# Expert retrieval of a diffusion block: 32 tokens times four expert ranks in a slot, and the V sum through 128x32 factors

## The reference, cut to what matters

```python
scores = jnp.einsum("blhtd,htkd->blhtk", q, sub_keys)
sv, si = lax.top_k(scores, PEER_TOPK)
cand_s = (sv[..., 0, :, None] + sv[..., 1, None, :]).reshape(b, L, PEER_HEADS, n_cand)
cand_i = (si[..., 0, :, None] * N_KEYS + si[..., 1, None, :]).reshape(b, L, PEER_HEADS, n_cand)
top_s, pos = lax.top_k(cand_s, PEER_TOPK)
idx = jnp.take_along_axis(cand_i, pos, axis=-1)
gate = jax.nn.softmax(top_s, axis=-1)
...
act = jax.nn.gelu(jnp.einsum("tkd,td->tk", u_tab[it], xt))
return jnp.einsum("tk,tkd->td", gt * act, v_tab[it])
```

## Time and profile before

| | |
|---|---|
| times of three runs | 5720.74, 5721.03, 5723.74 us, median 5721.03 |
| the profiled execution | 5723.5 us of span, and nothing of its time is listed outside it |
| PE busy | 4492.1 us, 78% |
| DVE busy | 3507.4 us, 61% |
| POOL busy | 2171.7 us, 38% |
| ACT busy | 1461.2 us, 26% |
| gathers (queue 0) | 1342.26 MB of 1549.20 MB moved |
| PE products of line 1510 | 5120 passes, 2619.8 us |

### The profile page before, as it was taken

How to read it: one execution, slowest core, us unless ns; L and a number is a source line. 1 busy time by engine, 2 the same in 40 slices (tenths; PEclk the granted TensorE clock), 3 DMA queues, 4 the chain that set the end, 5 groups by cost and what they waited for, 6 DMA issues and landing times. The chain is left out here.

```text
span 5723.5 us, 53344 instructions
## 1 busy us (share of the span) xinstructions
PE 4492.1 (78%) x15560; PEld 2613.2 (46%) x15560; DVE 3507.4 (61%) x7342; ACT 1461.2 (26%) x3249; POOL 2171.7 (38%) x1631
## 2 busy tenths in 40 slices
PE   9778979867777877777777777978986777777776
PEld 3677867743333533333333235777862333333332
DVE  1555565456666456666766667747336666666766
ACT  0244343222211312221222223334221222222222
POOL 0345323344444334444444443333323444444443
PEclk9888989888888888888888887898988888888888
DMA  8423202289999379999999992101219999999998
GB/s 310 150 82 116 74 1 96 89 312 386 371 385 378 151 309 383 378 384 382 377 386 380 384 384 102 61 30 67 81 63 382 383 378 382 382 387 383 385 384 330
DMA packets 232302, 1549.20 MB, mean 271 GB/s; under 512 B 39877, under 2 KB 41157, under 8 KB 45893
## 3 DMA queue, kind: packets, MB, share of 16 engines
q0 software_dynamic: 184320, 1342.26, 59.5%
q1 hardware_dynamic: 47818, 204.82, 10.3%
HBM read 1544.79 MB, written 2.20 MB: 270 GB/s over the span
## 5 line engine op out<-in xcount | busy, mean ns | idle before, releaser
L1510 PE MATMUL banks<-arena 128*128 128x512 f32 x5120 | 2619.8, 672 | 913.6 <-ACT arena L1486 913.1
L1419 POOL DMA_INDIRECT arena<-in_experts,arena x1280 | 1455.6, 1137 | 2114.5 <-PE banks L1510 1855.0
L1510 PEld LDWEIGHTS banks<-arena 128*128 128x128 f32 x5120 | 1077.7, 216 | 2457.0 <-issue 1288.4
L1450 DVE CUSTOM_DVE_ANT_0 arena<-arena 128x1024 f32<-128x1024 f32 x1280 | 1538.8, 1224 | 954.5 <-DMA arena<-in_experts,arena 925.5
L265 POOL TENSOR_TENSOR wide_low<-wide_blocks,wide_high 128x1024 fp32r<-128x1024 f32 x244 | 612.7, 2533 | 1182.3 <-ACT wide_high L255 1182.3
L1478 ACT ACTIVATE arena<-arena 128x4 f32<-128x4 f32 x320 | 66.1, 207 | 2659.4 <-DVE arena L1450 2659.4
L303 PE MATMUL banks<-activation_a,wide_high 128*128 128x512 f32 (+1 forms) x1568 | 582.9, 372 | 12.2 <-ACT arena L327 4.2
L305 PE MATMUL banks<-activation_a,wide_low 128*128 128x512 f32 (+1 forms) x1568 | 563.3, 359 | 0.0
L1486 ACT ACTIVATE arena<-identity,arena 128x128 f32<-128x128 f32 x1280 | 408.8, 390 | 100.2 <-DVE arena L1456 96.1
L304 PE MATMUL banks<-activation_b,wide_high 128*128 128x512 f32 (+1 forms) x1056 | 385.4, 365 | 0.0
L303 PEld LDWEIGHTS banks<-activation_a,wide_high 128*128 128x128 f32 x1568 | 308.7, 197 | 61.1 <-ACT arena L327 5.4
(11 more groups left out here) (176 smaller groups left out, 4576.6 us busy)
## 6 DMA issues: line engine op xcount, KB each, us to landing
wide_blocks<-in_wide SPq DMA_DIRECT2D x170, 1024.0 KB, 4.8
arena<-in_experts,arena POOLq DMA_INDIRECT x1280, 9.2
arena<-mod_rows SPq DMA_DIRECT2D x9, 512.0 KB, 5.4
residual<-in_tokens SPq DMA_DIRECT2D x6, 512.0 KB, 7.3
arena<-in_keys SPq DMA_DIRECT2D x3, 1024.0 KB, 7.2
arena<-in_icnt_grid SPq DMA_DIRECT2D x2, 1024.0 KB, 5.8
out_x<-residual SPq DMA_DIRECT2D x4, 512.0 KB
arena<-in_pool_w SPq DMA_DIRECT2D x3, 512.0 KB, 3.3
```

Of the source, the lines that this page charges most:

```text
L1419: pool.indirect_dma_start(out=v.ring[:, j % RING], out_offset=None, in_=io["experts"], in_offset=bass.IndirectOffsetOnAxis(ap=idx[:, par * ...
L1450: last = nc.vector.tensor_tensor_reduce(out=u_row, in0=u_row, in1=v.h2[:, t], scale=1.0, scalar=0.0, op0=ALU.mult, op1=ALU.add, accum_out= ...
L1510: mm = nc.tensor.matmul(k.ps[:, a + half], v.diag[:, j % 8], v.ring[:, j % RING, D + half * BANK:D + (half + 1) * BANK], start=False, stop ...
```

## The change

A slot no longer holds one rank of 128 tokens. It holds 32 tokens times four ranks: partition 32q + i of slot j in a group is token 32j + i with rank 4s + q, where s is the group. Group and unit counts stay: 16 gathers of 1 MB in a unit.

- **Token copies.** The dot product now needs the tokens of a slot repeated four times. PE makes these copies by products with slices of the identity (four 128x32 products of 512 columns for each of 8 half copies), ACT copies them from PSUM (`copies`), once for each tile: the first at the start of a stage, the next ones after the last group of a tile.
- **V sum.** The factor of a slot is 128x32: `masks` (a fold of the identity times the gates, made by POOL once for a unit) scaled by the Gelu on ACT. Slot j of a group writes PSUM partitions 32j to 32j + 31. For each half the four slots follow each other. One increment after the eight products frees all four slots. The zeroing and closing products (lines 1504 and 1515) go.
- **DVE** no longer multiplies gates and Gelu, and no longer waits for ACT after each group. The multiplication with the key numbers (line 1254) moves to POOL (`match`), after its fourth gather; `masks` stands after its eighth.
- **Numbers and gates in the new layout.** `spread` on PE brings them to the slot layout: 16 products 128x32 with 8 columns. It stands after the products of group 0 of each unit. Then `take_rows` on DVE writes the row indices of the next unit, right after the fourth dot product of group 0, and `take_gates` on ACT copies the gates.
- **Distance.** Choosing runs two units ahead instead of one: best keys after the sixth dot product, best pairs after the tenth, weights after the thirteenth. `stage_queries` chooses units 0 and 1.
- The loops are written out. The three rows loaded by SP have a place of their own in the arena. One more constant (`fold`) is loaded at the start.

```diff
-    ring, h2, scores, dg, small = carve(k, RING * 2 * D, 4 * D, 4 * 2048 + 256, 8 * P, 2000)
+    ring, h2, scores, lhs, small, rows = carve(k, RING * 2 * D, 4 * D, 4 * 2048, 8 * QUAD, 2080, 3 * D)
     v.ring = ring.rearrange("p (s c) -> p s c", s=RING)
     v.raw_ring = ring
     v.h2 = h2.rearrange("p (t c) -> p t c", t=4)
-    v.scores, v.g2, v.lng, v.lnb = scores, k.rows[:, 0], k.rows[:, 1], k.rows[:, 2]
-    v.diag = dg.rearrange("p (s c) -> p s c", s=8)
+    v.rows = rows.rearrange("p (n c) -> p n c", n=3)
+    v.scores, v.g2, v.lng, v.lnb = scores, v.rows[:, 0], v.rows[:, 1], v.rows[:, 2]
+    v.lhs = lhs.rearrange("p (q j c) -> p q j c", q=2, j=NJ)
...
+    def softmax(act, u):
+
+        act.wait_ge(k.top_ready.sem, b0["top_ready"] + u + 1)
+        nc.scalar.activation(raw, tv, ACT.Exp, bias=nmax, accum_out=esum).then_inc(k.soft_done.sem, 1)
+
+    def weigh(dve, u):
+
+        dve.wait_ge(k.soft_done.sem, b0["soft_done"] + u + 1)
         nc.vector.reciprocal(einv, esum)
         dve.drain()
-        g = gate[:, par * 16:par * 16 + 16]
-        nc.vector.tensor_scalar(g, g, einv, None, ALU.mult)
-
-    def softmax(act, par, unit):
-        act.wait_ge(k.top_ready.sem, unit + 1)
-        nc.scalar.activation(gate[:, par * 16:par * 16 + 16], tv, ACT.Exp, bias=nmax,
-                             accum_out=esum).then_inc(k.soft_done.sem, 1)
+        nc.vector.tensor_scalar(sel[:, u % 2, 1], raw, einv, None, ALU.mult)
+
+    def match(pool, u):
+
+        pool.wait_ge(k.picked.sem, b0["picked"] + u + 1)
+        nc.gpsimd.tensor_tensor(hot, hot, sif[:, u % 2].unsqueeze(1).to_broadcast(wide_shape), ALU.mult) \
+            .then_inc(k.matched.sem, 1)
+
+    def number(dve, u):
+
+        dve.wait_ge(k.matched.sem, b0["matched"] + u + 1)
+        nc.vector.tensor_reduce(sel[:, u % 2, 0], hot.rearrange("p s z b -> p s (z b)"), AX_X, ALU.add) \
+            .then_inc(k.chosen.sem, 1)
+
+    def spread(pe, u):
+
+        pe.wait_ge(k.chosen.sem, b0["chosen"] + u + 1)
+        if u >= 1:
+            pe.wait_ge(k.gate_copied.sem, b0["gate_copied"] + u)
+        for j in range(NJ):
+            for q in range(NJ):
+                last = nc.tensor.matmul(k.ps[q * QUAD:(q + 1) * QUAD, 7, j * 8:j * 8 + 8],
+                                        k.ident[:, j * QUAD:(j + 1) * QUAD], sel[:, u % 2, :, q * 4:q * 4 + 4],
+                                        start=True, stop=True)
+        last.then_inc(k.spread.sem, 1)
+
+    view = k.ps[:, 7, 0:NJ * 8].rearrange("p (j z s) -> p z s j", j=NJ, z=2)
+
+    def take_rows(dve, u):
+
+        dve.wait_ge(k.spread.sem, b0["spread"] + u + 1)
+        nc.vector.tensor_scalar(idx[:, u % 4], view[:, 0], float(layer * N_EXPERTS), None, ALU.add) \
+            .then_inc(k.idx_ready.sem, 1)
+
+    def take_gates(act, u):
+
+        act.wait_ge(k.idx_ready.sem, b0["idx_ready"] + u + 1)
+        if u >= 2:
+            act.wait_ge(k.masks_ready.sem, b0["masks_ready"] + u - 1)
+        nc.scalar.copy(gate[:, u % 2], view[:, 1]).then_inc(k.gate_copied.sem, 1)
+
+    def masks_of(pool, u):
+
+        pool.wait_ge(k.gate_copied.sem, b0["gate_copied"] + u + 1)
+        if u >= 1:
+            pool.wait_ge(k.lhs_ready.sem, b0["lhs_ready"] + 4 * u)
+        shape = [P, TOPK, QUAD]
+        nc.gpsimd.tensor_tensor(masks, k.fold[:].unsqueeze(1).to_broadcast(shape),
+                                bc(gate[:, u % 2].rearrange("p s j -> p (s j)"), shape), ALU.mult) \
+            .then_inc(k.masks_ready.sem, 1)
...
@@ stage_retrieve
+            for u in range(UNITS):
+                pool.wait_ge(k.idx_ready.sem, b0["idx_ready"] + u + 1)
+                for n in range(TOPK):
+                    g = u * TOPK + n
+                    if g >= RING:
+                        pool.wait_ge(k.slot_free.sem, b0["slot_free"] + (g - RING) // NJ + 1)
+                    pool.indirect_dma_start(
+                        out=v.ring[:, g % RING], out_offset=None, in_=io["experts"],
+                        in_offset=bass.IndirectOffsetOnAxis(ap=c.idx[:, u % 4, n // NJ, n % NJ:n % NJ + 1], axis=0),
+                    ).then_inc(k.landed[g % RING].sem, 16)
+                    if n == 3 and u >= 1 and u + 1 < UNITS:
+                        c.match(pool, u + 1)
+                    if n == RING - 1 and u >= 1:
+                        c.masks(pool, u)
...
-                            dve.wait_ge(k.gelus.sem, i * 8 + (q0 + t * 32 + par * 4 + q + 1))
-                            nc.vector.tensor_tensor(wgt[:, j - 3:j + 1], gel[:, j - 3:j + 1],
-                                                    gate[:, par * 16 + j - 3:par * 16 + j + 1], ALU.mult) \
-                                .then_inc(k.weights.sem, 1)
...
+            for u in range(UNITS):
+                t = u // PEER_HEADS
+                ahead = u + 2 < UNITS
+                for n in range(TOPK):
+                    g = u * TOPK + n
+                    if u % PEER_HEADS == 0 and n < NJ:
+                        dve.wait_ge(k.copy_ready.sem, k.copy_ready.at(t * 2 * NJ + 2 * n + 2))
+                    dve.wait_ge(k.landed[g % RING].sem, r0 + 16 * (g // RING + 1))
+                    if g >= 32 and n % NJ == 0:
+                        dve.wait_ge(k.lhs_ready.sem, b0["lhs_ready"] + (g - 32) // NJ + 1)
+                    u_row = v.ring[:, g % RING, 0:D]
+                    last = nc.vector.tensor_tensor_reduce(
+                        out=u_row, in0=u_row, in1=k.copies[:, n % NJ], scale=1.0, scalar=0.0,
+                        op0=ALU.mult, op1=ALU.add, accum_out=c.act_in[:, g % 32:g % 32 + 1])
+                    if n % NJ == NJ - 1:
+                        last.then_inc(k.dots.sem, 1)
+                    if n == 1 and u >= 1 and u + 1 < UNITS:
+                        c.number(dve, u + 1)
+                    if n == 3 and u >= 1 and u + 1 < UNITS:
+                        c.take_rows(dve, u + 1)
+                    if n == 5 and ahead:
+                        c.best_keys(dve, u + 2)
+                    if n == 9 and ahead:
+                        c.best_pairs(dve, u + 2)
+                    if n == 12 and ahead:
+                        c.weigh(dve, u + 2)
...
-                                nc.scalar.activation(v.diag[:, j % 8], k.ident[:], ACT.Copy,
-                                                     scale=wgt[:, j:j + 1]).then_inc(k.diags.sem, 1)
...
+            def copies(t):
+
+                for j in range(NJ):
+                    for half in range(2):
+                        n = (t * NJ + j) * 2 + half
+                        act.wait_ge(k.copy_proj.sem, k.copy_proj.at(n + 1))
+                        if t >= 1:
+                            act.wait_ge(k.dots.sem, b0["dots"] + t * PEER_HEADS * 4)
+                        nc.scalar.copy(k.copies[:, j, half * BANK:(half + 1) * BANK], k.ps[:, 4 + n % 2]) \
+                            .then_inc(k.copy_ready.sem, 1)
+
+            copies(0)
+            for u in range(UNITS):
+                t = u // PEER_HEADS
+                for q in range(4):
+                    g = u * 4 + q
+                    act.wait_ge(k.dots.sem, b0["dots"] + g + 1)
+                    a = (g % 8) * NJ
+                    nc.scalar.activation(c.gel[:, a:a + NJ], c.act_in[:, a:a + NJ], ACT.Gelu_apprx_tanh)
+                    if q == 0:
+                        act.wait_ge(k.masks_ready.sem, b0["masks_ready"] + u + 1)
+                    if g >= 2:
+                        act.wait_ge(k.slot_free.sem, b0["slot_free"] + g - 1)
+                    act.drain()
+                    for j in range(NJ):
+                        last = nc.scalar.activation(v.lhs[:, g % 2, j], c.masked[:, q * NJ + j], ACT.Copy,
+                                                    scale=c.gel[:, a + j:a + j + 1])
+                    last.then_inc(k.lhs_ready.sem, 1)
+                    if q == 0 and u >= 1 and u + 1 < UNITS:
+                        c.take_gates(act, u + 1)
+                    if q == 2 and u + 2 < UNITS:
+                        c.softmax(act, u + 2)
+                if u % PEER_HEADS == PEER_HEADS - 1 and t + 1 < NT:
+                    copies(t + 1)
...
-                        for half in range(2):
-                            mm = nc.tensor.matmul(k.ps[:, a + half], v.diag[:, j % 8],
-                                                  v.ring[:, j % RING, D + half * BANK:D + (half + 1) * BANK],
-                                                  start=False, stop=False, skip_group_check=True)
-                        mm.then_inc(k.slot_free.sem, 1)
...
+            def copies(t):
+
+                for j in range(NJ):
+                    for half in range(2):
+                        n = (t * NJ + j) * 2 + half
+                        if n >= 2:
+                            pe.wait_ge(k.copy_ready.sem, k.copy_ready.at(n - 1))
+                        for q in range(NJ):
+                            last = nc.tensor.matmul(k.ps[q * QUAD:(q + 1) * QUAD, 4 + n % 2],
```

(41 more changed lines are left out.)

222 lines of the change are left out of this document (89 added, 133 removed).

## The result

The changed kernel takes 5951.85 us (median of 4 runs, 5944.67 to 5952.71), the one before 5720.89; the ratio is **1.0405**, 95% interval 1.039 to 1.0419.

What follows compares the result with a forecast made beforehand. The prediction took a slot's way from row landed to slot free as the bound, not PE's work. A unit of 54.2 us against 43.9 gave 5723.5 + 762 + 24 + 90 + 15, about 6620 us; range 6000 to 7300.

Steps and rivals of the forecast that it cites:

- the chain through spread, group 1 and group 3: Waits from group 0's fourth dot product to the next unit's, summed to 54.2 us a unit against 43.9 before.
- X: PE time for a group's eight V-sum products: 5.6 us as 9 steps, only partly overlapped; 0.47 chance.
- floor of 5.5%: Most that can be won: gathers at 2.50 us make a unit 40.0 us, so 3.9 us less, 312 us in all.
- tiles fully together: Rival for a group's V-sum products: all four column tiles overlap, products take 3.4 us, total 6210 us; chance 0.20.
- links (a) and (c): Group 0's fourth dot product to group 1's first, 12.1 us; group 1's last dot product to group 3's gathers, 7.0 us.
- Y: PE time for spread's 16 products, 32 passes: 3.7 us, between 2.7 and 8.2.
- Refill 16.5: Link (d), from the first new gather's issue to group 3's fourth dot product: 16.5 us, between 14.9 and 18.0 seen.
- Link (e), 10.0: The next unit's group 0 lands behind group 3: four gathers at 2.5 us each, 10.0 us.
- It does them in idle time: POOL's two new passes, 1.3 us each a unit, fit its 1855 us idle time; without that cover 208 us.
- Tile ends: Token copies at tile ends, 7 times, delay group 0 by 12.9 us each: 90 us, or 24 with full overlap.
- The threshold: With fixed parts of 22.8 us, a unit stays under 43.9 when 2X + Y + refill is under 21.1; faster had 0.07.
- the six units without spread: First and last units of a stage: a loop of 24.6 us plus choosing, some 4 us a unit over before, 24 us.

Runs made afterwards that it cites:

- two ways of removing it: Changed kernel with take_rows moved behind the eighth dot product and take_gates to group 1: 5839.28 us; or with spread ahead of group 0's products: 5819.44 us.
- the run with one tile: Changed kernel with all four slots of a group summed into the same column tile, output not the block's: 7165.58 us, 1.2522 of the kernel before.
- slot by slot: Changed kernel with both halves of a slot next to each other instead of products half by half: 6077.46 us, 1.0607 of the kernel before.
- the small masks: Changed kernel with POOL's masks pass cut from 16 to 2 ranks except in a stage's first unit, output not the block's: 5896.21 us.
- the same work one step earlier: Changed kernel with take_rows and take_gates late, plus best keys and best pairs each one dot product earlier: 5769.57 us, 1.0074 of the kernel before.
- the run with the spares alone: Changed kernel with five unread spare PE products after each group, nothing else changed: 5944.08 us, 1.0378 of the kernel before.

## Why the prediction was wrong

**What held.** Slower; the chain through spread, group 1 and group 3; the reason (time from landed to freed, not PE's work); DVE's new wait, shown by two ways of removing it; that a longer X is paid more than once in a unit (the prediction had two payments, the run with one tile showed three); and no version went below its floor of 5.5%.

**The step that failed: X = 5.6, "product k + 1 can only overlap the second pass of product k".** It measured 3.4. The step took it that a product waits until the second pass of the one ahead of it has begun, even where their tiles differ. It does not: slot by slot, with both products of a tile next to each other, the span stayed at 3.4 us, and with one tile for all, `spread`'s passes for the free tiles started before the last product ahead of them (3029.62 and 3030.04). The program order of starts, which the prediction cites for its 5.6, does not hold across tiles in this trace. This was the rival "tiles fully together", given 0.20. In links (a) and (c) that is 2 x 2.2 = 4.4 us of the 8.4 by which the unit was off. The Trainium skill (TensorEngine Tiling (Array Packing), Theoretical Speedup) says up to four times where the small dimension is at most 32; 16 passes at 0.86 would be 13.8 us and took 3.4, so the trace agrees.

**The second failed term: Y = 3.7, bounds 2.7 to 8.2.** It measured 0.6, outside both: 3.1 us. The bounds took one pass after another from rows with one tile; in four tiles 32 passes of 8 columns overlap. The same error in another term, and no rival had it.

**Refill 16.5.** 14.2 in the mean (link (d)): 2.3 us. In the kernel before, where PE spread the issues out, the same stretch took 16.7. That the burst is the reason is not shown.

**Link (e), 10.0.** 11.8 in the mean, 1.8 us more, and it was 12.0 before: rows did not land 2.5 us apart through this stretch. This error had the other sign.

**Left out.** The masks as a loop of their own and the dot product slowed beside POOL's pass (some 0.7 us a unit by the small masks: 46.7 - 46.0). "It does them in idle time" was wrong for one of two passes. This error too had the other sign.

**Tile ends.** Predicted 7 x 12.9 = 90, or 24 with full overlap. The seven units across a tile's end took 50.8 us and the other 70 took 46.5, 4.4 more; before it was 44.9 and 43.9, 1.0 more. That is 7 x 3.4 = 24, as the rival had it.

With X 3.4, Y 0.6 and refill 14.2 the prediction's own sum gives 54.2 - 4.4 - 3.1 - 2.3 = 44.4 a unit; with 0.7 for POOL and 1.8 in link (e) it is 46.9, and 47.0 was measured. At 44.4 the forecast would still have been slower, by 1 to 2%, so the direction did not hang on the errors. The threshold does not stand up: 2X + Y + refill came to 21.6, just above the 21.1 at which the sign was to turn, but the fixed parts, put at 22.8, came to 25.4. The range missed because its lower end, full overlap with Y 2.7 and refill 14.9, took both for floors, and neither was one. The DMA share, expected near 0.8, fell only to 0.92, as the unit stayed at 46.7. One sum is off by itself: for the six units without spread the loop of 24.6 gives 2 x 24.6 = 49.2, 5.3 over before and not some 4, which is 32 us for the six instead of 24.

## What to carry to other kernels

Where a ring of buffers feeds the engines, count the time from "landed" to "free" in units of one transfer before counting anybody's busy time: here PE got 1405 us lighter and the kernel 231 us slower. One engine's wait for another inside that stretch cost some 110 to 130 us of it (both ways of removing it), and giving slots back four at a time cost the kernel before 13.6%. Work put shortly ahead of the last step of a batch delays the batch; the same work one step earlier cost 0.9 us a unit less. And a bound taken from instructions that ran one after another is no lower bound for instructions that may run side by side.

## What the runs showed of the hardware

- Four column tiles of 32 work together in fp32, both passes of each product: 16 passes in 3.4 us at the lower clock. In one tile they took 8.59 us, four of them at the lower clock and twelve at the higher. 32 passes of 8 columns on four tiles took 0.6 us.
- A pass for a free tile starts ahead of an earlier one for a busy tile: at 3029.62 and 3030.04 in the run with one tile, and in the same way in 73 of its 74 units.
- The granted clock of the retrieval stages was 0.58 to 0.59 in the changed kernel and 0.87 before. Spare products that nobody reads raised it to 0.89 and 0.96, and made the kernel before 1.0% faster. After 6.93 us of idle time a group's products started at the lower level again, in the run with the spares alone (2729.79).
- A dot product on DVE takes 1.22 us alone. Beside POOL's masks pass the median was 1.73 (62 of them in the changed kernel, 1.22 to 2.69); beside its match pass most took 1.23, the longest 2.94, and one is shown with 2.67 (at 2698.93 in the run with spares alone).
- DVE can see an increment by PE 2 us after the last product's recorded end, depending on what stands before or after it in PE's order; the cause is open.
